# Two networks in one kernel: attention on eight PSUM banks in a new order, gates by tanh, the recurrence's output in three pieces

## What is computed

```
h = rms_norm(x, attn_norm[i]);  proj = h @ w_in[i]           # 1024 -> 2304 (q,k,v) + 3072 (gates)
ya = softmax attention, 4 heads of 64, causal
yb = attention with a window of 128 and a sink per head, 8 query heads, 2 key heads
yc = differential attention, 4 heads: (softmax(q1 k1) - lam * softmax(q2 k2)) @ v, then rms_norm
g  = sigmoid(gates)                                          # 3 x 1024
x  = x + (g0*(ya @ w_pa) + g1*(yb @ w_pb) + g2*(yc @ w_pc)) @ w_out
x  = x + (silu(gate_u) * val_u) @ w_down                     # u = conv(rms_norm(x) @ w_up)
```

```
gate_branch, rec = split(x @ w_in);  u = conv4(rec);  r, i = sigmoid(block-diagonal products of u)
a = exp(-8 r softplus(-lam));  h_t = a_t h_{t-1} + sqrt(1 - a^2) (i u)
out = (h * gelu(gate_branch)) @ w_o
```

## Time and profile before

| | |
|---|---|
| median of 3 runs | 2211.56 us (2209.94 to 2212.55) |
| the profiled execution's own time | 2214.4 us |
| its span, first to last instruction | 2212.6 us |
| TensorE busy (matmul) | 2139.2 us, 97% |
| TensorE weight load busy | 1923.3 us, 87% |
| VectorE busy | 1390.9 us, 63% |
| ScalarE busy | 1092.1 us, 49% |
| GpSimd busy | 134.3 us, 6% |
| mean granted TensorE clock | 0.987 |
| DMA | 377.95 MB, mean 171 GB/s |

### The profile page before, as it was taken

The page is one execution under the profiler, slowest core; times in us unless marked ns, Lnnn a source line. Parts: engine busy times, 40 slices in busy tenths (PEclk is TensorE's granted clock), DMA queues, the critical chain, the costliest instruction groups (busy, mean ns, idle before and its releaser), DMA issues.

```text
span 2212.6 us, 31455 instructions
## 1 busy us (share of the span) xinstructions
PE 2139.2 (97%) x13601; PEld 1923.3 (87%) x13607; DVE 1390.9 (63%) x1478; ACT 1092.1 (49%) x1263; POOL 134.3 (6%) x80
## 2 busy tenths in 40 slices
PE   6998999999899999999999989999999999999998
PEld 5988899889889998988899888998889989888997
DVE  4855687676567666656655586555766557465554
ACT  4564555456736554444544465444555444454543
POOL 1101010020011002200000000000000004000000
PEclk9999999999999999999999999999999999999999
DMA  6523565554255555544565545655446555545653
GB/s 225 179 95 115 171 200 184 178 187 132 78 171 172 190 184 177 200 159 136 191 208 190 176 152 166 204 187 152 154 152 209 184 179 181 177 158 182 200 186 113
DMA packets 252931, 377.95 MB, mean 171 GB/s; under 512 B 14085, under 2 KB 195578, under 8 KB 252794
## 3 DMA queue, kind: packets, MB, share of 16 engines
q1 hardware_dynamic: 251884, 374.57, 51.9%
q10 hardware_dynamic: 910, 1.38, 0.2%
HBM read 374.87 MB, written 1.05 MB: 170 GB/s over the span
## 4 chain that ended last, share of the span: by engine, by line
PE 81%; ACT 7%; DVE 6%; DMA 3%; DVEq 2%; issue 1%; POOL 0%; SPq 0%; ACTq 0%; POOLq 0%
PE bank L695 53%; PE acc L695 26%; ACT slot_hi L1350 3%; DVE slot_lo L1782 2%; PE bank L693 2%; ACT arena L1411 2%; DVEq L1777 2%; ACT arena L1345 1%; DMA slot<-in_mlp_w 1%; DMA slot<-in_w_in 1%; DMA slot<-in_w_out 0%; ACT split L1378 0%; DVE arena L2338 0%; DMA slot<-in_lru_w_in 0%; POOL arena L2531 0%
## 5 line engine op out<-in xcount | busy, mean ns | idle before, releaser
L1782 DVE TENSOR_TENSOR slot_lo<-slot,slot_hi 128x2048 fp32r<-128x2048 f32 (+1 forms) x344 | 802.3, 2339 | 407.4 <-ACT slot_hi L1350 406.2
L695 PE MATMUL bank<-split,slot_hi 128*128 128x256 f32 x5496 | 1010.3, 286 | 8.2 <-DVE arena L1852 4.4
L695 PEld LDWEIGHTS bank<-split,slot_hi 128*128 128x128 f32 x5496 | 871.4, 194 | 21.4 <-issue 12.2
L1350 ACT ACTIVATE slot_hi<-slot 128x2048 fp32r<-128x2048 f32 (+1 forms) x344 | 652.5, 1902 | 317.5 <-DMA slot<-in_mlp_w 135.6
L695 PE MATMUL bank<-split,slot_lo 128*128 128x256 f32 x2748 | 782.7, 285 | 0.0
L695 PE MATMUL acc<-slot_hi,split 128*128 128x512 f32 x1904 | 610.6, 394 | 10.2 <-DVE split L2082 5.1
L695 PEld LDWEIGHTS bank<-split,slot_lo 128*128 128x128 f32 x2748 | 532.4, 194 | 0.0
L695 PEld LDWEIGHTS acc<-slot_hi,split 128*128 128x128 f32 x1904 | 360.9, 190 | 86.7 <-DVE split L2082 5.5
L695 PE MATMUL acc<-slot_lo,split 128*128 128x512 f32 x952 | 373.9, 393 | 0.0
L695 PE MATMUL bank<-slot_hi,split 128*128 128x512 f32 (+1 forms) x880 | 267.9, 382 | 12.1 <-DVE slot_lo L1782 5.2
L1345 ACT ACTIVATE arena<-bank 128x512 f32<-128x512 f32 (+2 forms) x199 | 110.8, 573 | 336.8 <-PE bank L695 322.2
(11 more groups left out here) (198 smaller groups left out, 1053.9 us busy)
## 6 DMA issues: line engine op xcount, KB each, us to landing
slot<-in_mlp_w SPq DMA_DIRECT2D x128, 1024.0 KB, 5.3
slot<-in_ret_w_in SPq DMA_DIRECT2D x48, 1024.0 KB, 5.2
slot<-in_w_up SPq DMA_DIRECT2D x40, 1024.0 KB, 5.2
slot<-in_w_in SPq DMA_DIRECT2D x38, 1024.0 KB, 5.3
slot<-in_w_down SPq DMA_DIRECT2D x22, 1024.0 KB, 4.9
slot<-in_ret_w_o SPq DMA_DIRECT2D x16, 1024.0 KB, 5.0
slot<-in_lru_w_in SPq DMA_DIRECT2D x10, 1024.0 KB, 7.0
slot<-in_w_out SPq DMA_DIRECT2D x8, 1024.0 KB, 4.9
```

The lines of the kernel that those rows point to most:

```text
L695: i = nc.tensor.matmul(o, w, m, start=start, stop=stop)
L1350: A(whi[u.r][:, 0:u.cols], raw[u.r][:, 0:u.cols], ACT.Copy).then_inc(slot_hi[u.r], 1)
L1782: TTO(wlo[u.r][:, 0:u.cols], raw[u.r][:, 0:u.cols], f32(whi[u.r][:, 0:u.cols]), ALU.subtract)\
```

## The change

- The ring gets eight banks from the second pair of projections of a layer to the end of its last probabilities: the four old ones and the four of the accumulator. After that it is four again. Before the first product into the accumulator TensorE waits for the readers of the borrowed banks.
- TensorE's order in the attention becomes: gates 0-2, transposes, (layer 0: parameter transposes), gate 3, scores 0-3, gates 4 and 5, scores 4-7, group 0, gates 6 and 7, scores 8-11, group 1, gates 8 and 9, scores 12-15, group 2, scores 16-19, gate 10, group 3, transposes of the results, gate 11, group 4. The last transposes of results move from ahead of the second branch to between its second and third bank.
- Gates: tanh of half the argument in place of sigmoid; VectorE multiplies by (gate + 1), and the missing half is applied when the merged rows are split.
- Splits in the attention are placed one by one ("through" a slot) and in another order on ScalarE and VectorE; VectorE takes the first branch's products in two pairs around the norm of the differential heads.
- Start: the ten parameter loads and the positions move from ScalarE to SP, behind the fifth slot; the first slot is split before the first rows are.
- Recurrence: the two gate tables are loaded behind the fifth slot instead of the third; output in three pieces (rows 0-1, 2-5, 6-9), with scans, products and splits interleaved.

```diff
 NSLOT, SLOT = 5, 2048
 AHEAD = 3
-NBANK = 4
+NBANK, NSUM = 8, 4
...
+    def use(self, width, key=None):
+
+        if key is not None:
+            self.left[key] = [u for r, u in self.latest.items() if r >= width]
+        self.width, self.at = width, 0
...
-        r = len(self.made) % self.n
+        r = self.at % self.width
+        self.at += 1
...
+        bank += [acc[:, tt, h * 512:(h + 1) * 512] for tt in range(TT) for h in range(HALVES)]
...
+            def through(self, u):
+                self.upto(u.seq)
...
+                    if i == 4 and L == 0:
...
+                        for l in range(DEPTH):
...
+                                sp.dma_start(dst, src).then_inc(V["rows_loaded"], 16)
+                        sp.dma_start(posi[:, :], I["positions_2"].to_broadcast([P, S])).then_inc(V["pos_loaded"], 16)
...
-                if c == 2:
+                if c == 4:
 
                     sp.wait_ge(V["tab_free"], tabs["lg", 0].uses + 1)
...
+            def sum_banks_left(key):
+                for u in banks.left[key]:
+                    evacuated(pe, u)
...
                 gates([3])
                 in_sbuf(f"qk{L}", range(7))
                 softmax_scores(f"s{L}", range(4), pairs)
-                gates([4])
+                gates([4, 5])
                 softmax_scores(f"s{L}", range(4, 8), pairs)
-                gates([5])
                 probs(0, [0, 1, 2, 3], 0)
-                gates([6])
+                gates([6, 7])
                 softmax_scores(f"s{L}", range(8, 12), pairs)
                 probs(1, [4, 5, 6, 7], 4)
-                gates([7])
+                gates([8, 9])
                 softmax_scores(f"s{L}", range(12, 16), pairs)
                 probs(2, [8, 9, 10, 11], 8)
-                gates([8])
                 softmax_scores(f"s{L}", range(16, 20), pairs)
-                gates([9])
+                gates([10])
                 probs(3, [12, 13], 12)
-                gates([10])
                 in_sbuf(f"y{L}", range(3))
                 for i in range(3):
                     transposes(banks[f"yt{L}", i], y1, 2 * i)
+                gates([11])
                 probs(4, [14, 15], 14)
-                gates([11])
...
+                sum_banks_left(f"att{L}")
...
                     A(col(N_STD + tt), col(N_VAR + tt), ACT.Sqrt).then_inc(V["std_ready"], 1)
+                    if n == 0 and tt == 0:
+                        weights.upto(0)
                     hi_rows(name, tt)
...
-                         func=ACT.Sigmoid)
+                         func=ACT.Tanh, scale=0.5)
...
+                gate_split(7)
+                softmax(0)
+                act.wait_ge(V["lam_in"], L + 1)
+                A(col(LAM_E, 2), col(LAM, 2), ACT.Exp).then_inc(V["lam_exp"], 1)
+                gate(4)
+                gate_split(8)
+                gate(5)
+                turned((0, 1, 2, 3), 0)
+                gate_split(9)
+                softmax(1)
+                gate(6)
+                gate_split(10)
+                gate(7)
+                turned((4, 5, 6, 7), 1)
+                gate_split(11)
+                softmax(2)
+                gate(8)
+                weights.through(slots[f"w_p{L}", 0])
+                gate(9)
+                turned((8, 9, 10, 11), 2)
+                softmax(3)
+                weights.through(slots[f"w_p{L}", 1])
+                gate(10)
+                turned((12, 13), 3)
+                softmax(4)
+                for i in range(3):
+                    hi_part(f"yt{L}", i, yT1)
+                gate(11)
+                turned((14, 15), 4)
+                weights.through(slots[f"w_p{L}", 2])
...
+                weights.through(slots[f"w_p{L}", 3])
+                weights.through(slots[f"w_out{L}", 0])
                 hi_part(f"yt{L}", 3, yT1)
-                for c in (2, 3):
-                    weights.ahead(slots[f"w_p{L}", c])
+                weights.through(slots[f"w_out{L}", 1])
...
+                    STT(out=(mt1 if b else mrg)[:, f, :],
+                        in0=gat[:, 8 * b + 2 * f:8 * b + 2 * f + 2, :].rearrange("p a s -> p (a s)"), scalar=1.0,
+                        in1=bank[u.r][:, :], op0=ALU.add, op1=ALU.mult).then_inc(bank_read[u.r], 1)
...
+            scans((0, 1))
+            weights.ahead(slots["lw", 7])
             dve.wait_ge(V["lru_gelu"], 1)
+            gated(0)
+            scans((2, 3))
+            low_rows(0)
+            scans((4, 5))
             for c in (6, 7):
                 evacuated(dve, banks["lw", c])
-            scans(0)
+            gated(1)
             inputs(1)
-            weights.ahead(slots["lw", 7])
-            low_rows(0)
+            low_rows(1)
+            scans(range(6, 10))
             for c in (8, 9):
                 evacuated(dve, banks["lw", c])
-            scans(1)
+            gated(2)
             weights.ahead(slots["lw", 8])
-            low_rows(1)
+            low_rows(2)
```

More of the change, by code:

```diff
@@ L291, in plan @@
         bank("lw", [c])
-    for g in range(2):
+    for g in range(3):
         his.take("lru", g)
@@ L1459, in gate @@
                 def gate(n):
-                    weights.ahead(slots[f"w_in{L}", 9 + n])
                     u = banks[f"g{L}", n]
@@ L1470, in turned, with gate_split @@
                         copy(pt1[:, g % 2, i, :], bank[u.r][:, 0:MAP], u)
-                for n in range(3):
-                    gate(n)
+                def gate_split(n):
+                    weights.through(slots[f"w_in{L}", 9 + n])
+                gate_split(3)
+                gate(0)
+                gate_split(4)
+                gate(1)
+                gate_split(5)
+                gate(2)
                 for i in range(0, 7, 2):
@@ L1926, in heads, with gate_split @@
                     d()
-                def gates_ahead(*ns):
-                    for n in ns:
-                        weights.ahead(slots[f"w_in{L}", 9 + n])
+                def gate_split(n):
+                    weights.through(slots[f"w_in{L}", 9 + n])
                 for i, c in enumerate(c for pair in PAIRS for c in pair):
@@ L2057, in _ @@
                     lo_part(f"yt{L}", i, yT1)
+                weights.through(slots[f"w_p{L}", 1])
                 values(4, (14, 15))
-                gates_ahead(11)
                 d()
@@ new lines, in _ @@
+                gated(1, 0)
+                gated(1, 1)
+                weights.through(slots[f"w_out{L}", 0])
+                gated(1, 2)
+                lo_part(f"yt{L}", 3, yT1)
+                gated(1, 3)
+                weights.through(slots[f"w_out{L}", 1])
+                for f in range(4):
+                    dve.wait_ge(V["branches_added"], L * 4 + (1 + f))
+                    gated(2, f)
+                    d()
+                    TTO(mrg[:, f, :], mrg[:, f, :], mt1[:, f, :], ALU.add).then_inc(V["merge_added"], 1)
+                    if f:
+                        lo_merged(f - 1)
@@ L2104, in _ @@
                 lo_merged(3)
-                weights.ahead(slots[f"w_p{L}", 3])
                 for c in range(3):
```

178 lines of the change are left out of this document (83 added, 95 removed).

## The result

| | before | after |
|---|---|---|
| median | 2211.07 us (2209.94 to 2212.55, 4 runs) | 2159.05 us (2158.19 to 2160.24, 4 runs) |
| the profiled execution's own time | 2214.4 | 2158.19 |
| its span | 2212.6 | 2156.4 |
| TensorE busy | 2139.2 | 2111.0 |
| TensorE idle (span less busy) | 73.4 | 45.4 |

The ratio is 0.9763, with a 95% interval of 0.9748 to 0.9779: 52 us less by the medians, where 46 were forecast. On another chip the changed kernel gave 2159.45 (last experiment). In the two profiled executions TensorE's idle time falls by 28.0 us. The span falls by 56.2, because TensorE also does its work at the high level of its clock for longer.

What follows compares the result with a forecast made beforehand. TensorE bounds the kernel, so only its idle time and lost clock count: 19.6 + 18.1 + 1.0 + 2.4 + 7.0 = 48.1, less 2.1 gives 46; 2214.4 becomes 2168.4, with medians 2.8 lower 2165.6 us, range 2158 to 2186.

Steps and rivals of the forecast that it cites:

- Attention, layer 0: Attention: banks, order and tanh leave 1.5 us of waits per layer; gain 19.6 us in layer 0, 18.1 in layer 1.
- The start and what stands before the attention: From kernel start to layer 0's attention: first rows and first product come earlier; 2.4 us gained.
- The cap: Before layer 0's attention: VectorE's roped rows end at 91.18, TensorE takes them at 92.23, so at most 1.05 us gained.
- the 0.5 for the small loads: Start: eleven small loads moved to SP's queue were taken to cost 0.5 us of delay.
- The recurrence: Recurrence: waits on weight slot (3.1) and output (3.4) go, waits on taps grow to 6.0; gain 7.0 us.
- The clock's term: Recurrence: clock fall at the wait on VectorE's taps costs 1.7 to 3.4 us, taken as 2.6.
- The allowance of 2.1 for a margin that fails: Taken off the summed gain for one short clock fall at a margin called positive: 2.1 us.
- The clock stays low: Rival, 14%: in both attentions the clock falls in longer rows without a gate; gain 28, 2184 us.
- VectorE binds: Rival, 14%: VectorE's margins of 0.2 to 2 us fail in four places per layer; 19 back, 2185 us.
- The small loads clog the queue: Rival, 8%: at the start, moved loads delay the slot TensorE takes up at 56.66 by 10 us; 2176 us.
- In-order splits: Rival "slower", 3%: in attention, ScalarE's exponentials stand behind splits whose data is late; 67 lost against 46, 2233 us.
- Tables not shared: Rival, 3%: tanh and exp use different ScalarE tables, so 22 loads stay; about 8 on the path, 2174 us.

Runs made afterwards that it cites:

- a1: Kernel before plus only the ring of eight banks in the attention: 2189.78 us, 22.0 us faster.
- d2: Changed kernel with the old start put back: 2161.14 us, 2.1 us slower.
- a2: Kernel before plus only the new start: 2211.75 us, ratio 1.0001 to before.
- e1: Changed kernel again, unedited, on another chip: 2159.45 us.
- a4: Kernel before plus only tanh in place of sigmoid for the gates: 2200.38 us, 11.4 us faster.
- c1: Changed kernel with VectorE's splits of the recurrence's sixth and seventh input slots moved behind the convolution taps: 2154.13 us, 4.9 us faster.
- c2: c1 plus the fifth slot split ahead of the first taps on ScalarE and VectorE: 2152.46 us, 6.6 us below the changed kernel.
- b2: Changed kernel with sigmoid gates put back: 2161.89 us, 2.8 us slower.
- a3: Kernel before plus only the recurrence's edits: 2201.43 us, 10.4 us faster.
- d1: Kernel before plus eight banks, tanh, start and recurrence, but not the new attention order: 2172.78 us.

## Why the prediction was right

The forecast of 46 us had the sign, the mechanism and nearly every place; the result, 52 or 2159.05, lies at the lower edge of its range (2158 to 2186). By its own steps:

- **Attention, layer 0: 19.6 forecast, 20.7 found; layer 1: 19.1 and 21.5.** No wait on a copied gate, the waits around the difference 0.5, the merged low half 1.1 late where 0.7 was said, clock 1.00. TensorE's idle time and the clock's share account for 19.5 and 19.3 of what was found; the other 1.2 and 2.2 are not broken down. One step was misread and cost nothing in the sum: the 2.2 us wait of the earlier trace rows was put to the chain of the difference; a1 shows that it was a wait for a free bank, which eight banks alone remove. What the banks are worth alone was therefore expected at less than half of what a1 measured.
- **The start and what stands before the attention: 2.4 forecast, 4.6 found.** First rows at 8.8 and first product at 14.9, as forecast; no wait near 54. Along TensorE's list the lead over before is 2.9 us at the first product. It grows by 0.2 where the clock rises, by 0.3 where the parameter transposes stood, by 0.6 with a wait of 0.38 for a slot (56.7 in before) and by 1.5 with the wait of 1.29 at 64.0. So it is 5.5 at the first query transpose (86.7 for 92.2), and the parameter transposes take 0.9 back, as forecast. Two terms were mis-sized. The cap, "only 1.05 us can be gained before VectorE binds", does not hold: VectorE's roped rows end at 86.67 where the earlier trace rows had 91.18, because its chain starts from TensorE's projections and moves with them. All but the start gives 3.1 here (d2 against before), the start 1.5. And the 0.5 for the small loads: in the changed kernel TensorE does not wait for that slot, and in a2, where it comes 3.0 us earlier, it waits 0.6 longer than in before.
- **The recurrence: 7.0 forecast, 8.0 found.** The waits on the taps are 0.5, 3.8 and 0.6, 4.9 in all (4 and 2 were said), and none on the output. The clock's term was 1.7 to 3.4, taken as 2.6; it was 3.4 in the changed kernel's first trace and 5.1 in e1's, so its upper bound was too low.
- **Retention and MLP between: 0 forecast, 1.5 found.** It is clock: before had a fall of 1.7 at 1009, after two waits of 0.73 each, and the changed kernel has the same pair of waits (960.5 and 961.9) and no fall. The forecast took the falls for fixed to their waits; they are not (below), and this gain is luck.
- **The allowance of 2.1 for a margin that fails** was not needed: no margin failed by more than the low half's 0.4 us, and no fall stood behind it.
- **The rivals.** "The clock stays low" in long rows without a gate: 1.00 in both attentions. "VectorE binds": only the 1.1 us of the merge. "The small loads clog the queue": the slot behind the token loads took 12.0 us to land where it took 13.59 in the earlier trace rows. By the Trainium skill ("DMA: Bandwidth & Descriptors", Queues, rings and completion order) the eleven loads stand in front of the sixth slot. They were issued by 17.1 us, the sixth slot only at 27.3 (it landed in 5.0 us) and the one behind the token loads at 33.5, so nothing of the rule shows here. "In-order splits": none stood in front of an exponential long enough to make TensorE wait. "Tables not shared": 22 loads became 10.

The 6 us of the miss: the stretches gave 8.1 more than forecast, the allowance 2.1, and the step from the two profiled executions to the medians takes 4.2 off. The change is not a sum of parts: the same tanh is worth 11.4 us in the old order and 2.8 at most in the new, the same banks 22.0 and 16.2, the same start nothing and 2.

## What to carry to other kernels

Where one engine does 97% of the work, read each of its waits down to the line of the releaser and ask whether it waits for a result or for room: room (here banks) is bought by one edit, a result by another order. What an edit beside the path is worth is measured in the kernel that it will be in: tanh was worth 11.4 us ahead of the other edits and no more than 2.8 behind them. Where a stall goes with a lower clock its removal can return more than twice its length (a wait of 2.9 us and 3.4 of clock in before), but a few microseconds of that are dealt anew in every execution.

## What was not expected of the hardware

The falls of TensorE's clock are bound to waits, but loosely. Over the 14 profiled executions of this study TensorE waits 57 times for 2 us or more between 40 and 2140 us, and in 48 of these waits or within 5 us of their ends the granted clock drops to 0.50 for a cost of 1.7, 3.4 or 5.1 us. Of six single waits of 1.33 to 1.57 us five go with such a fall, the four of a4 and the one of c1; the one of 1.41 in c2 does not. Of 33 single waits of 1.0 to 1.3 us one is followed by a fall, with a wait of 1.56 right behind it. Of 28 pairs of 0.73 us waits, 1.4 us apart, three are (1009 in before, 964 in b2, 1922 in d2). Here is one such pair in before, and the same pair in the changed kernel (length, busy of PE, granted clock, DMA share, GB/s):

```profile
1005.00:1025.00 20.00, 18.36 (x83) 0.91 0.38 118
```

```profile
955.00:975.00 20.00, 18.36 (x105) 1.00 0.37 126
```

Both are busy for 18.36 of 20 us. The Trainium skill ("TensorE: Matmul & The Clock Gate", Part 1: The HAM clock gate) says that the activity monitor runs freely and isn't reset when a kernel starts. That would make the same wait meet a fall in one execution and none in another, and a shift of the whole program could change which ones. The runs agree with this (a3, d1), but none isolates it. Whatever the reason, a few microseconds of this kernel's time can't be forecast from one trace.

The clock's rise at the start varies too. The first products take 0.63 us each and start 0.43 apart; later ones of the same size take 0.39 and start 0.23 apart (before):

```profile
20.93 0.63 PE L695 MATMUL bank<-slot_lo,split 128*128 128x512 f32 x1
...
23.25 0.39 PE L695 MATMUL bank<-slot_lo,split 128*128 128x512 f32 x1
```

A table load costs ScalarE its own 1.283 us and no more in these traces: in c2 one begins at 1225.40, 0.02 after the split before it ended (1223.47 + 1.91), and the next activation begins 0.01 after its end.
